# Turning gathered token rows on VectorE instead of TensorE in a mixture-of-experts decoder kernel

## The reference, cut to what matters

```python
def swiglu(h, w_gate_up, w_down):
    g, u = jnp.split(h @ w_gate_up, 2, axis=-1)
    return (jax.nn.silu(g) * u) @ w_down

def moe_ffn(h, router, w_gate_up, w_down):
    ...
    logits = (t @ router).astype(jnp.float32)
    top_v, top_i = lax.top_k(logits, TOP_K)
    gates = jax.nn.softmax(top_v, axis=-1)
    combine = jnp.sum(jax.nn.one_hot(top_i, N_EXPERTS, dtype=jnp.float32) * gates[..., None], axis=1)
    out = jnp.zeros_like(t)
    for e in range(N_EXPERTS):
        out = out + combine[:, e:e + 1].astype(t.dtype) * swiglu(t, w_gate_up[e], w_down[e])
    return out.reshape(B, S, D)
```

## Time and profile before

| | us |
|---|---|
| median of 3 runs | 1431.83 |
| lowest, highest | 1431.61, 1432.95 |
| the profiled execution's own time | 1432.99 |
| its span, first to last instruction | 1431.2 |
| its mean granted TensorE clock | 0.996 |
| TensorE busy | 1423.2 (99%) |
| VectorE busy | 1200.1 (84%) |
| ScalarE busy | 964.0 (67%) |
| GpSimd busy | 98.7 (7%) |

### The profile page before, as it was taken

One profiled execution on the slowest core, in us unless ns is written; L12 is line 12 of the kernel. 1 busy time (PEld: TensorE's weight loads), 2 busy tenths in 40 slices (PEclk: granted clock), 3 DMA queues, 4 the chain that ended last, 5 costly groups with the idle time before them and its releaser, 6 DMA issues.

```text
span 1431.2 us, 19930 instructions
## 1 busy us (share of the span) xinstructions
PE 1423.2 (99%) x6790; PEld 1197.1 (84%) x6790; DVE 1200.1 (84%) x1106; ACT 964.0 (67%) x838; POOL 98.7 (7%) x146
## 2 busy tenths in 40 slices
PE   9999999999999999999999999999999999999999
PEld 9998888888988888888888888888888888888887
DVE  6486888877686698988988988898898889898897
ACT  7465444444684577777777777777777777777775
POOL 3010000000022020000000000000000000000000
PEclk9999999999999899999999999999999999999999
DMA  9454655565345699999999999999999999999995
GB/s 333 146 183 141 221 191 176 185 210 167 110 149 192 237 382 392 374 374 393 381 367 393 390 351 397 390 373 372 393 380 365 394 395 351 396 392 373 378 393 199
DMA packets 212591, 442.93 MB, mean 309 GB/s; under 512 B 16372, under 2 KB 56760, under 8 KB 212544
## 3 DMA queue, kind: packets, MB, share of 16 engines
q1 hardware_dynamic: 208640, 430.18, 82.4%
q0 software_dynamic: 3888, 12.13, 2.8%
q10 hardware_dynamic: 16, 0.00, 0.0%
HBM read 434.88 MB, written 7.37 MB: 309 GB/s over the span
## 4 chain that ended last, share of the span: by engine, by line
PE 96%; DVE 2%; ACT 1%; issue 0%; POOL 0%; DVEq 0%; POOLq 0%; ACTq 0%
PE PS L1715 21%; PE PS L1716 21%; PE PS L1719 21%; PE PS L1423 5%; PE PS L1424 5%; PE PS L1425 5%; PE PS L1154 4%; PE PS L1210 2%; PE PS L1202 2%; PE PS L1204 2%; PE PS L1261 1%; PE PS L1267 1%; PE PS L1264 1%; PE PS L1184 1%; PE PS L1704 1%; PE PS L1707 1%
## 5 line engine op out<-in xcount | busy, mean ns | idle before, releaser
L1869 DVE TENSOR_TENSOR wlo<-ring,whi 128x2048 fp32r<-128x2048 f32 x334 | 763.9, 2292 | 96.6 <-ACT whi L793 94.5
L793 ACT ACTIVATE whi<-ring 128x2048 fp32r<-128x2048 f32 x334 | 640.5, 1919 | 186.5 <-PE PS L1719 176.4
L1715 PE MATMUL PS<-whi,xhi 128*128 128x512 f32 x864 | 340.8, 394 | 0.0
L1716 PE MATMUL PS<-whi,xlo 128*128 128x512 f32 x864 | 336.6, 390 | 0.0
L1719 PE MATMUL PS<-wlo,xhi 128*128 128x512 f32 x864 | 231.0, 389 | 0.0
L1719 PEld LDWEIGHTS PS<-wlo,xhi 128*128 128x128 f32 x864 | 162.1, 188 | 33.9 <-DVE wlo L1869 0.2
L1716 PEld LDWEIGHTS PS<-whi,xlo 128*128 128x128 f32 x864 | 162.4, 188 | 32.3
L1715 PEld LDWEIGHTS PS<-whi,xhi 128*128 128x128 f32 x864 | 162.3, 188 | 32.4
L1715 PE MATMUL PS<-whi,hhi 128*128 128x512 f32 x440 | 171.9, 391 | 0.0
L1716 PE MATMUL PS<-whi,hlo 128*128 128x512 f32 x440 | 171.3, 389 | 0.0
L1719 PE MATMUL PS<-wlo,hhi 128*128 128x512 f32 x440 | 117.8, 390 | 0.0
(11 more groups left out here) (377 smaller groups left out, 1618.5 us busy)
## 6 DMA issues: line engine op xcount, KB each, us to landing
ring<-in_moe_w_gate_up SPq DMA_DIRECT2D x448, 512.0 KB, 6.7
ring<-in_moe_w_down SPq DMA_DIRECT2D x224, 512.0 KB, 6.6
ring<-in_dense_w_gate_up SPq DMA_DIRECT2D x56, 512.0 KB, 4.5
ring<-in_dense_w_down SPq DMA_DIRECT2D x28, 512.0 KB, 4.4
ring<-in_a_w_in SPq DMA_DIRECT2D x12, 768.0 KB, 7.2
ring<-in_mem_w_kv SPq DMA_DIRECT2D x4, 1024.0 KB, 6.0
ring<-in_a_w_out SPq DMA_DIRECT2D x4, 1024.0 KB, 5.2
ring<-in_b_w_out SPq DMA_DIRECT2D x4, 1024.0 KB, 4.8
```

The lines of the kernel that those rows point to most:

```text
L793: nc.scalar.activation(whi[:, j, :], ring[:, h * SLOT:(h + 1) * SLOT], ACT.Copy).then_inc(S("highs"), 1)
L1715: mm(out_, lhsT=xh, rhs=whi[:, j, c0:c0 + HD], start=begin, stop=False)
L1716: mm(out_, lhsT=xl, rhs=whi[:, j, c0:c0 + HD], start=False, stop=False)
L1869: v.tensor_tensor(wlo[:, j, :], ring[:, h * SLOT:(h + 1) * SLOT], whi[:, j, :].bitcast(F32), ALU.subtract).then_inc(S("lows"), 1)
```

## The change

From the third expert on (experts 2 to 7, whose rows are gathered while experts 1 to 6 run), TensorE no longer turns the rows. VectorE does it in squares of 32 x 256: each instruction turns eight blocks of 32 x 32 from 32 tokens of `xs` to 32 partitions of `xsT`, a part of the SBUF tile `xT`. There are 16 instructions, in three lumps: 6 after VectorE's low parts in block 4, 5 after those in block 5, 5 at the end of block 6. ScalarE and VectorE read `xsT` in SBUF instead of the PSUM banks for `xhi` and `xlo`. So that the rows are there in block 4, the list of tokens is copied in block 3 instead of 5, and the list of rows to add to in block 2 instead of 4; for expert 1's rows, gathered during expert 0, everything stays.

```diff
--- before.py
+++ after.py
@@ -327,6 +327,7 @@
         put_at = arena[:, o:o + NT][0:CAP]; o += NT
         pause3 = arena[0:1, o:o + 1]; o += 1
         xs, ys = xn[0:CAP, 0], xn[0:CAP, 1]
+        xsT = xT[:, :, 0:CAP]
 
 
         NORMS = ["x0", "mem", "mq0", "mk0", "hm", "mk1", "x1", "x2", "ckv", "cq", "mq1", "kh", "qh0", "qh1", "qh2", "x3a", "x3b"]
@@ -740,7 +741,7 @@
 
                 nc.scalar.activation(ys, PS[0:CAP, 4:6, :].rearrange("p a n -> p (a n)"), ACT.Copy, scale=gate[:, 0:1]).then_inc(S("y_out"), 1)
 
-            def x_high(i):
+            def x_high(i, by_vector=False):
 
                 if is_first(i):
                     for half, (there, done) in enumerate((("half_gathered", "half_xhi"), ("gathered", "xhi_ready"))):
@@ -749,8 +750,8 @@
                                              ACT.Copy).then_inc(S(done), 1)
                     return
                 act.wait_ge(S("gathered"), i + 1)
-                nc.scalar.activation(xhi[:, :, xe_], PS[:, 6:8, 0:4 * CAP].rearrange("p a (k n) -> p a k n", n=CAP),
-                                     ACT.Copy).then_inc(S("xhi_ready"), 1)
+                src = xsT if by_vector else PS[:, 6:8, 0:4 * CAP].rearrange("p a (k n) -> p a k n", n=CAP)
+                nc.scalar.activation(xhi[:, :, xe_], src, ACT.Copy).then_inc(S("xhi_ready"), 1)
 
             def hi_of(n, r=None):
 
@@ -821,7 +822,7 @@
                             expert_hi(i, b + 1, 0)
                         expert_hi(i, b + 1, 1)
                 if not last:
-                    x_high(i + 1)
+                    x_high(i + 1, by_vector=not first)
 
             def mem_softmax(l, bank):
 
@@ -1756,7 +1757,7 @@
                 first = is_first(i)
                 for b in range(NBE):
                     expert_gate_up(i, b, (lambda: turn_expert(NB + 1)) if first and b == 1 else None)
-                    if b == 6 and not last:
+                    if b == 6 and first:
                         pe.wait_ge(S("rows_in"), i * 16 + 16)
                         turn_rows()
                     if b > 0:
@@ -1915,7 +1916,16 @@
                         part = v.tensor_scalar(Sx[:, t], iota, put_at[:, t:t + 1], None, ALU.is_equal)
                     part.then_inc(S("dispatch"), 1)
 
-            def gathered(i):
+            def turn_rows(squares):
+
+                for n in squares:
+                    (r, c), last = divmod(n, 4), n == 15
+                    done = v.transpose(xsT[32 * c:32 * c + 32].rearrange("p k (q s) -> p k q s", q=4)[:, :, r, :],
+                                       xs[32 * r:32 * r + 32].rearrange("p (k q f) -> p k q f", k=KD, q=4)[:, :, c, :])
+                if last:
+                    done.then_inc(S("gathered"), 1)
+
+            def gathered(i, by_vector=False):
 
                 if is_first(i):
                     for half, (there, done) in enumerate((("half_xhi", "half_xlo"), ("xhi_ready", "xlo_ready"))):
@@ -1925,8 +1935,8 @@
                                         xhi[:, ks, xe_].bitcast(F32), ALU.subtract).then_inc(S(done), 1)
                     return
                 dve.wait_ge(S("xhi_ready"), i + 1)
-                v.tensor_tensor(xlo[:, :, xe_], PS[:, 6:8, 0:4 * CAP].rearrange("p a (k n) -> p a k n", n=CAP),
-                                xhi[:, :, xe_].bitcast(F32), ALU.subtract).then_inc(S("xlo_ready"), 1)
+                src = xsT if by_vector else PS[:, 6:8, 0:4 * CAP].rearrange("p a (k n) -> p a k n", n=CAP)
+                v.tensor_tensor(xlo[:, :, xe_], src, xhi[:, :, xe_].bitcast(F32), ALU.subtract).then_inc(S("xlo_ready"), 1)
 
             def expert(i, last=False):
                 first = is_first(i)
@@ -1947,9 +1957,9 @@
                     v.tensor_tensor(hnE, PS[0:CAP, expert_bank(i, b) + 1, :], silE, ALU.mult).then_inc(S("h_ready"), 1)
                     if first and b == 2:
                         gates()
-                    if b == (6 if first else 4):
+                    if b == (6 if first else 2):
                         next_dispatch(i, last)
-                    if b == 5 and not last:
+                    if b == (5 if first else 3) and not last:
                         if not first:
                             dve.wait_ge(S("fetching"), i)
                         dve.wait_ge(S("raw_in"), i * 16 + 32)
@@ -1960,8 +1970,12 @@
                         if b > 0 or not first:
                             expert_lo(i, b + 1, 0)
                         expert_lo(i, b + 1, 1)
+                    if b >= 4 and not first and not last:
+                        if b == 4:
+                            dve.wait_ge(S("rows_in"), i * 16 + 16)
+                        turn_rows({4: range(0, 6), 5: range(6, 11), 6: range(11, 16)}[b])
                 if not last:
-                    gathered(i + 1)
+                    gathered(i + 1, by_vector=not first)
 
             def sum_half(t, half):
```

## The result

The changed kernel took 1461.89 us (median of 4 runs, 1459.84 to 1462.67), the kernel before 1432.09 us beside it: a ratio of 1.0206, 95% interval 1.0193 to 1.0219. It is 29.8 us slower. The forecast was 1449.9 us, 18.1 us slower, in a range from 1440 to 1465.

The account below looks back on a forecast made before the run. TensorE's own pace was taken to bound the kernel. Six boundaries at 3.03 us net, the 0.91 saved included, made it 18.1 us slower: 1431.83 + 18.1 = 1449.9 us, range 1440 to 1465.

Parts of the forecast that it names:

- rival 2: TensorE's waits of 2.5 and 1.3 us at each boundary bring the clock to 0.50: 1456 or 1480 us; chance 0.13.
- short falls: At each boundary, a low-clock stretch mostly covering the second wait costs 1 us, 6 in all: 1456 us.
- the forecast's own case of a full clock: Squares of 0.43 to 0.50 us and granted clock 1.00 throughout: 1449.9 us, chance 0.65.
- TensorE's saving of 0.91 us a boundary: Eight transposes leave TensorE in each of experts 1 to 6: 6 x 0.91 = 5.5 us gained.
- The price of a square: On VectorE, a 32x256 square costs 0.45 us, with ends at 0.27 and 0.63.
- Lumps one and two absorbed: Squares in blocks 4 and 5 leave VectorE 2.64 us late as block 6 begins, without stalling TensorE.
- the edge: At block 6's cut 2, VectorE's low part has 3.20 us of room, less 0.16 for hand-over, before TensorE stalls.
- Lump three on the path: Five squares behind block 6's hidden product delay x_high and the next expert's first cut: 3.03 us net a boundary.
- The clock: In the expert stage the granted clock stays at 1.00 throughout, so waits add no slower matmuls.
- long ones: At each boundary, a low stretch of the same ten us at half pace costs 5 us, 30 in all: 1480 us.
- Moves at no cost: List copy in block 3, scatter wait in block 2, ring refills and SBUF reads of xhi and xlo: nothing added.
- Rivals 1, 3 and 4: Square price 0.63 us (chance 0.12); quick squares, 0.16 us (0.06 with lower prices); boundary with more cover (gain 0.02, break-even 0.02).

Follow-up runs that it names:

- early signal: Changed kernel without its sixteen squares, a one-column copy in block 5 giving the signal x_high waits for: 1427.27 us, ratio 0.9963 to the kernel before.
- the run with ten squares: Changed kernel with the third lump joined to the second, 6 squares in block 4, 10 in block 5, none in block 6: 1439.24 us, ratio 1.0052.
- the late signal without squares: Changed kernel without its sixteen squares, a one-column copy behind block 6's hidden product giving the signal x_high waits for: 1432.88 us, ratio 1.0004.
- dead squares: Kernel before, TensorE still turning the rows, with the changed kernel's sixteen squares and moved copies added, their output unread: 1439.76 us, ratio 1.0051.

## Why the prediction was right, and where it fell short

The direction, the place and the size of the loss at full clock were forecast; one term, the clock, was left out. The measured time lies in the range, but through what rival 2 described (the range's upper end was drawn for its short falls, and for most of the double price), and not through the forecast's own case of a full clock. (Six times 3.03 us is 18.2; the recorded sum has 18.1.)

**TensorE's saving of 0.91 us a boundary.** Right. Without squares and with an early signal the kernel is 5.2 us faster (0.9963); forecast 5.5.

**The price of a square.** 0.45 us, as forecast. The reasoning from the 32x128 squares and the one-column copy held. The sixteen squares of one 128x1024 f32 tile take about 7.1 us here, 0.89 us for each 128x128. The Trainium skill gives 311 ns for a bf16 tile of 128x128 (VectorE: DVE Perf Modes, "The three transpose paths"). That figure doesn't carry over to f32 in these squares. The Trainium skill's rule is to turn 128x128 on TensorE where PSUM will do as the destination (VectorE: DVE Perf Modes, "Rules for kernel authors"). The runs neither bear it out nor refute it: TensorE pays 0.91 us for all eight, but with room on VectorE the squares are free.

**Lumps one and two absorbed.** Right: no wait in blocks 5 and 6, and the run with ten squares found the edge where it was placed.

**Lump three on the path, 5.42 us behind it.** Right: from the last square's end (1322.75 + 2.24) to the `wlo` matmuls at 1330.26 it was 5.27 us, where 5.33 was forecast, the 5.42 less 0.09 for the slower start. The first of the changed boundaries, which had no low clock ahead of it, took 121.41 us from one expert's first `wlo` matmuls to the next expert's, here in the changed kernel:

```profile
591.60 1.08 PE L1708 MATMUL PS<-wlo,xhi 128*128 128x512 f32 x4
```

```profile
713.01 2.08 PE L1708 MATMUL PS<-wlo,xhi 128*128 128x512 f32 x4 [1.13 <-DVE wlo L1870]
...
714.89 1.91 PE L1711 MATMUL PS<-whi,xlo 128*128 128x512 f32 x4
```

against 118.44 before, 2.97 us more where 3.03 was forecast. The waits, 2.31 and 1.13 us, are the 2.5 and 1.3 forecast less the overlapping end of the last matmul. With the clock held up, the sum of six was 17.9 us for 18.1.

**The clock: the step that failed.** The sum carried it at nothing, and "granted clock 1.00 throughout" was expected; rival 2 had it at 0.13. A 0.50 in the expert stage was the prediction's own sign of being wrong, and it came at all six boundaries. The mechanism was named, but its argument against, a wait of 0.77 us that left the clock up, said nothing about one three times as long. It measured about 12 us, 2 us a boundary, between the rival's short falls (6 us) and long ones (30 us). It should have been weighed more: the forecast itself put two gaps of 2.5 and 1.3 us, 0.9 us apart, at each boundary, and in the earlier trace rows the clock was at 0.50 in a stretch that TensorE was busy for the whole of.

**Moves at no cost.** Right: the squares never waited for the rows, and the scatter was never waited for. The same held with the list copied in block 2 and the first squares in block 3.

**Rivals 1, 3 and 4** fell: the squares start 0.45 us apart, not 0.63 or 0.16, and the boundary had just the cover that was read, as the late signal without squares shows.

## What to carry to other kernels

Before moving work to an engine with idle time, ask not only whether it fits but who stands behind its last piece. The kernel became 30 us slower with five of sixteen squares ahead of a signal that a third engine waits for, and about 5 us faster with the same squares one block earlier; in such a place even the signal alone used up the gain. And where a forecast puts a wait on TensorE as long as the 2.3 us here, the matmuls behind it need a price at the lower clock as well. Waits of 1.1 us needed none; no run here lies between.

## What the runs showed of the hardware that was not expected

A single wait of 2.3 us between dense matmuls was followed or accompanied by a stretch at 0.50 of the clock at each of six boundaries, in both kernels that had it unfilled; single waits of 0.7 to 1.1 us were not, in four kernels (filler in the first wait, dead squares, no squares with the late signal, ten squares in one lump). When the fall came relative to the wait varied from one boundary to the next. At the first boundary of the changed kernel it came within 712, in the second wait (TensorE started again at 713.01). At the fourth it came at the start of 1081, when the first wait wasn't over (it ended at 1081.29):

```profile
712.00:713.00 1.00, 0.00 (x0) 0.00 (x0) 1.00 (x2) 1.00 (x2) 0.00 (x0) 0.69 0.02 4
...
1081.00:1082.00 1.00, 0.71 (x2) 0.61 (x3) 0.73 (x1) 1.00 (x2) 0.00 (x0) 0.51 0.59 214
```

Twenty matmuls of 256 columns in the first wait took 2.57 us, 0.13 us each, and were enough to prevent it.
